# Dense down products with the two operands exchanged, summed into the same banks as the gathered rows, and tile 0 closed later

## What is computed

```python
def peer_ffn(xn, w_q, keys, U, V):
    ...                                  # top 16 of 128 x 128 product keys, 8 heads
    eidx = jnp.take_along_axis(cidx, sel, axis=-1)     # 128 experts of a token
    gate = jax.nn.softmax(top, axis=-1)
    def block(args):
        xb, eb, gb = args
        hid = jax.nn.gelu(jnp.einsum('nkd,nd->nk', U[eb], xb))
        return jnp.einsum('nk,nkd->nd', (hid * gb), V[eb])
```

## Time and profile before

| | us |
|---|---|
| median of 3 runs | 2242.39 |
| lowest, highest | 2233.48, 2247.92 |
| the profiled execution, device time | 2228.19 |
| its span, first to last instruction | 2226.1 |

### The profile page before, as it was taken

The page is one execution under the profiler, slowest core; times in us unless marked ns, Lnnn a source line. Parts: engine busy times, 40 slices in busy tenths (PEclk is TensorE's granted clock), DMA queues, the critical chain, the costliest instruction groups (busy, mean ns, idle before and its releaser), DMA issues.

```text
span 2226.1 us, 37936 instructions
## 1 busy us (share of the span) xinstructions
PE 2028.4 (91%) x13044; PEld 1240.7 (56%) x13044; DVE 1440.3 (65%) x3365; ACT 845.8 (38%) x2456; POOL 743.5 (33%) x658
## 2 busy tenths in 40 slices
PE   6998989989999888999989898899899997889997
PEld 5777768764444222444478776787544442234444
DVE  2425454569999898545542354744899989975545
ACT  1221222034545785433322203220444557853332
POOL 0400000025555676545312000000355457755552
PEclk9999999999999999999999999999999999999999
DMA  6330233658899999999753201436599999999995
GB/s 259 125 121 2 80 124 127 235 188 317 311 346 359 371 356 349 361 374 397 302 223 116 94 20 65 160 133 239 202 320 340 378 365 355 371 374 390 370 385 234
DMA packets 121546, 569.81 MB, mean 256 GB/s; under 512 B 42505, under 2 KB 44713, under 8 KB 61609
## 3 DMA queue, kind: packets, MB, share of 16 engines
q0 software_dynamic: 76032, 389.06, 46.6%
q1 hardware_dynamic: 43648, 175.12, 21.7%
q10 hardware_dynamic: 1696, 3.45, 0.4%
HBM read 725.63 MB, written 6.58 MB: 329 GB/s over the span
## 4 chain that ended last, share of the span: by engine, by line
PE 57%; DVE 24%; issue 9%; ACT 4%; DMA 4%; another core or an unknown queue 1%; POOL 0%; DVEq 0%; SPq 0%; ACTq 0%; POOLq 0%
PE ps L1059 12%; PE ps L978 11%; PE ps L585 10%; PE ps L648 7%; DVE arena L2019 6%; PE ps L936 3%; PE ps L905 3%; PE ps L919 3%; DMA arena<-in_uv,arena 2%; PE ps L1007 2%; DVE arena L2044 1%; DVE arena L1914 1%; DVE arena L1905 1%; DVE arena L1904 1%; DMA ring<-in_uv,arena 1%
## 5 line engine op out<-in xcount | busy, mean ns | idle before, releaser
L1471 POOL DMA_INDIRECT arena<-in_uv,arena x264 | 333.6, 1263 | 276.7 <-PE ps L978 237.7
L1471 POOL DMA_INDIRECT ring<-in_uv,arena x264 | 322.6, 1222 | 265.1 <-PE ps L978 219.2
L2019 DVE SCALAR_TENSOR_TENSOR arena<-arena 128x1024 bf16<-128x1024 f32 x264 | 319.4, 1224 | 113.1 <-DMA arena<-in_uv,arena 102.8
L2019 DVE SCALAR_TENSOR_TENSOR arena<-ring,arena 128x1024 bf16<-128x1024 f32 x264 | 320.2, 1225 | 111.7 <-DMA ring<-in_uv,arena 102.1
L978 PE MATMUL ps<-arena 64*64 64x512 f32 x2112 | 289.5, 619 | 46.6 <-ACT arena L1363 39.6
L978 PE MATMUL ps<-ring,arena 64*64 64x512 f32 x2112 | 291.0, 622 | 43.9 <-ACT arena L1363 39.0
L1361 ACT ACTIVATE arena<-arena 128x1 f32<-128x1 f32 x528 | 105.4, 200 | 494.7 <-DVE arena L2019 485.8
L1461 POOL COPY arena<-arena 128x8 uint32 (+1 forms) x66 | 37.1, 562 | 750.7 <-DVEq L1986 750.3
L1059 PEld LDWEIGHTS ps<-hold,ub 128*128 128x128 f32 x1024 | 180.5, 190 | 161.1 <-issue 143.6
L1059 PE MATMUL ps<-hold,ub 128*128 128x256 f32 x1024 | 268.9, 398 | 0.0
L648 PE MATMUL ps<-xn,ring 128*128 128x264 f32 x1024 | 246.1, 399 | 15.5 <-remote 12.8
(11 more groups left out here) (443 smaller groups left out, 2385.8 us busy)
## 6 DMA issues: line engine op xcount, KB each, us to landing
ring<-in_w SPq DMA_DIRECT2D x88, 1024.0 KB
ub<-in_uv SPq DMA_DIRECT2D x64, 512.0 KB
ub<-in_ud SPq DMA_DIRECT2D x48, 512.0 KB
hold<-in_ud SPq DMA_DIRECT2D x16, 512.0 KB, 6.0
ring<-in_uv,arena POOLq DMA_INDIRECT x264
arena<-in_uv,arena POOLq DMA_INDIRECT x264
hold<-in_st SPq DMA_DIRECT2D x2, 2048.0 KB
out_st<-hold SPq DMA_DIRECT2D x2, 2048.0 KB
```

Of the source, the lines that this page charges most:

```text
L1471: e.indirect_dma_start(out=row(k), out_offset=None, in_=A["uv"], in_offset=bass.IndirectOffsetOnAxis(ap=ix[:, par, k:k + 1], axis=0), **sk ...
L2019: stt(prod[:, n % 2, :], u, 1.0, xtok[:, tt, :], ALU.mult, ALU.mult, accum_out=hid[:, k:k + 1]).then_inc(S("dve_hid"), 1)
```

## The change

The down products exchange their operands: `hd` (64 or 128 tokens) becomes the weight and V moves with 512 columns, so that the result is token-major and goes to the banks of tile 0 (0, 1) and of tile 1 (2, 3), where the gathered rows are summed as well. In the bank of the second half the swapped halves ask for two products with 64 tokens each. A block is 6 products in four parts (`part` = 2 tt + half) in place of 8 in eight. Tile 0 stays open until the end of `down_slots`. The samples get banks 4 and 5, the sample sum at the end bank 6. `add_down`, the wait for `dve_xa` and the second opening of banks 0 and 1 go.

```diff
-SUM_BANK = (0, 2, 0)
+SUM_BANK = (0, 2, 4)
...
                     for s in range(n):
-                        if s == n - SLOT:
-                            e.wait_ge(S("dve_xa"), 1)
-                            open_sum(0, 1)
                         weighted(s % SLOT, 1 if s < n - SLOT else 2)
-                        for j, dt in [divmod(m_, KT) for m_ in range(s * DENSE * KT // n, (s + 1) * DENSE * KT // n)]:
-                            if dt == 0:
+                        for j, part in [divmod(m_, 2 * TT) for m_ in range(s * DENSE * 2 * TT // n, (s + 1) * DENSE * 2 * TT // n)]:
+                            if part == 0:
                                 take(e, w_full[j % UB], 16)
-                            m = mm(bank(4 + dt // 2, SEQ, SEQ * (dt % 2)), ub[:, j % UB, dt * P:dt * P + P], hd[:, j, :],
-                                   start=False, stop=False, skip_group_check=True)
-                            if dt == KT - 1:
+                            tt, half = divmod(part, 2)
+                            v = ub[:, j % UB, 512 * half:512 * half + 512]
+                            for q in range(1 + half):
+                                to = chunk(q) if half else slice(0, P)
+                                of = slice(tt * P + HD * (1 - q), tt * P + HD * (2 - q)) if half else slice(tt * P, tt * P + P)
+                                m = mm(ps[to, SUM_BANK[tt] + half, :], hd[:, j, of], v, start=False, stop=False, skip_group_check=True)
+                            if part == 2 * TT - 1:
                                 m.then_inc(w_free[j % UB], 1)
...
-                close_sum(0)
                 e.wait_ge(S("act_step"), step("act_it1"))
                 open_sum(2, 3)
-                gate_slots(1)
-                for half in range(2):
-                    turned(0, half, half + 1)
-                with e.Fori(0, 3) as i:
+                with e.Fori(0, 4) as i:
                     gate_slots(1)
...
-                open_sum(4, 5, 6, 7)
+                open_sum(4, 5)
                 down_slots()
-                mm(bank(7, 1), nothing, nothing[:, 0:1], start=False, stop=True, skip_group_check=True).then_inc(S("pe_step"), 1)
+                close_sum(0)
                 close_sum(2)
                 for k in range(SLOT):
                     weighted(k, 1)
+                    if k == 1:
+                        for half in range(2):
+                            turned(0, half, half + 1)
                     if k == 7:
                         sum_squares_first(l)
-                    if k == 3:
+                    if k == 4:
                         e.wait_ge(S("act_acc"), 4)
...
-                    if s == P + SLOT:
+                    if s == samples + 1:
                         sums_out(0, 1)
...
-                    if s == samples + 2:
+                    if s == samples + 3:
                         sums_out(2, 2)
...
-                    if s >= samples + 2 and s < samples + 6:
-                        add_down(s - samples - 2)
+                    if s in (samples + 4, samples + 5):
+                        add_turned(0, s - samples - 4, 1 + s - samples - 4)
```

More of the change, by code:

```diff
@@ L76 @@
 BIG = 3.0e38
-PE_STEPS = ("ket", "vt", "dl", "hy", "lr", "kk", "rk", "tr", "bv", "rot", "if", "rows", "svt", "sa", "po", "mean", "it0", "it1", "vd")
+PE_STEPS = ("ket", "vt", "dl", "hy", "lr", "kk", "rk", "tr", "bv", "rot", "if", "rows", "svt", "sa", "po", "mean", "it0", "it1")
 NORM_EPS, RWKV_EPS, HEAD_EPS = 1e-6, 64e-5, 1e-5
@@ L163 @@
 LATE = ("dve_hid pe_acc pe_xa act_acc act_top dve_top dve_route sp_sw sp_sr act_ps pe_ps pe_wq act_step pe_step "
-        "sp_out sp_fin sp_dfin dve_ix dve_xa").split()
+        "sp_out sp_fin sp_dfin dve_ix").split()
 ARENA = 22208
@@ L373, in build @@
                 "pe_cf pe_xt pe_cm pe_co pe_ctr pe_hh pe_ks pe_p pe_ps pe_s pe_sc pe_y pe_step pe_t pe_u pe_var pe_wo "
-                "pe_wq dve_hid pe_acc pe_xa act_acc dve_ix dve_xa "
+                "pe_wq dve_hid pe_acc pe_xa act_acc dve_ix "
                 "pool_hg pool_hy "
@@ L1104, in _ @@
                             from_ = NS // 2 * (kt // 4)
-                            m = mm(bank(0, NS, NS * kt), xtok[:, 2, kt * P:kt * P + P], C("group")[:, from_:from_ + NS], start=True, stop=True)
+                            m = mm(bank(6, NS, NS * kt), xtok[:, 2, kt * P:kt * P + P], C("group")[:, from_:from_ + NS], start=True, stop=True)
                         m.then_inc(S("pe_xa"), 1)
@@ L2064, in add_turned @@
                     own(i)
[L2066 to L2071, removed]
                 now = {}
@@ L2113, in _ @@
                         e.wait_ge(S("act_xt"), 3)
[L2114 to L2117, removed]
                     dot(s % P, s // P, s + (SLOT if s >= samples else 0), row_round + s // SLOT)
@@ L2120, in _ @@
                 e.wait_ge(S("pe_xa"), 3)
-                own(tt_(x[:, :, SEQ:N], x[:, :, SEQ:N], bank(0, NS * KT).rearrange("p (a b) -> p a b", b=NS), ALU.add))
+                own(tt_(x[:, :, SEQ:N], x[:, :, SEQ:N], bank(6, NS * KT).rearrange("p (a b) -> p a b", b=NS), ALU.add))
                 for half in range(2):
```

## The result

| | before | changed |
|---|---|---|
| median of 20 runs, us | 2235.4 | 2244.15 |
| lowest, highest | 2230.77, 2247.92 | 2235.35, 2251.02 |
| profiled execution's span | 2226.1 | 2234.2 |

The ratio is 1.0031, with a 95% interval of [1.0019, 1.0043]: slower by 0.3%, some 7 us (4 to 10). The forecast was +6.4 us, 0.3%, and 2248 in all. The 2248 stands 4 us above the median measured because it started from 2242.4, the median of three runs, and 20 runs of the kernel before have theirs at 2235.4. The medians differ by 8.75 us, the ratio says 7. A second measurement, with 10 runs of the changed kernel, gave 1.0022 [1.0002, 1.0042].

What follows compares the result with a forecast made beforehand. PE was taken to bound the down stage, DVE the gate stage and layer end. Terms 4.6 - 0.4 - 1.5 + 0.5 = +3.2 us a layer, +6.4 for two, gave 2248 us from 2242.4; range 2233 to 2264.

Steps and rivals of the forecast that it cites:

- What bounds the kernel: PE sets the down stage, full for 217.00 us; DVE sets the gate stage and the end of the layer.
- The down products: Down stage: 128 parts, wide ones at 1.06 us and pairs at 1.02, 133.1 in place of 128.5; +4.6 us a layer.
- the banks' opening: Down stage: the second opening of banks 0 and 1 leaves the middle of the stage; -0.4 us a layer.
- Rougher steps: Down stage: steps hold 1 or 2 parts where they had 2 or 3 products; costed at nothing.
- SP's clears: End of the layer: SP's 70 semaphore clears wait for tile 0's close, 11 us at most; costed at nothing.
- rows of V: Down stage: V blocks come at the same pace, with SP's queue unchanged there; no cost.
- The gate stage: Steps 96 to 167: tile 0's two additions leave DVE; -1.5 us a layer, bounds 0 and 1.69.
- The end of the layer: After the down products: DVE waits for tile 0's turned half, last dot at T + 10.55, before T + 10.07; +0.5 us.
- Serial pairs: Down stage: a pair's two products run one after the other, 1.90 us, 56 us more a layer, 2361 us; chance 0.04.
- A load showing in each pair: Down stage: each pair shows one more 0.13 us weight load, 8.4 us a layer, 2265 us; chance 0.06.
- Cheaper changes between neighbours of 128 rows: Down stage: form changes cost less, pair at 0.94, with DVE's full 1.69; -2.1 us a layer, 2238 us; chance 0.12.
- DMA as the bound: Down stage: DMA engines at 0.99 set it, hiding longer products and the gate stage's saving; 2242 us; chance 0.05.

Runs made afterwards that it cites:

- the kernel without the addition: Kernel before without tile 0's two additions in steps 142 and 143, the waits kept; down stage 217.82 us in both layers.
- fours: Kernel before with its own down products laid down in fours, 64 groups in place of 88; ratio 0.9969, stages 213.67 and 217.38 us.
- eights: Kernel before with the eight down products of a block in one group, 32 groups; ratio 0.9997, stages 216.15 and 217.69 us.

## Why the prediction was right, point by point

**What bounds the kernel.** As said. The control without a fifth of the traffic is the strongest sign: 221.85 us to the hundredth, with DMA at 0.91 in place of 0.98.

**The down products.** A 128-wide part was put at 1.06 and measured 1.06. The pair was put at 1.02 and measured 1.01. The term was +4.6 with the banks' opening of -0.4, together +4.2; measured 221.85 - 217.8 = +4.0 us in the first layer. In the second it was +2.4 by the profiles, where the old one had a first down step at half clock; the kernel without the addition gives that layer as 217.82, so +4.0 too. The clock of the old first steps of that layer:

```profile
1976.60:1981.00 4.40, 4.36 (x20) 1.62 (x20) 3.38 (x11) 1.69 (x6) 2.19 (x3) 0.61 1.03 406
```

Added up from start to start, the parts take 4.5 us more than the old products and the opening of the banks was 0.4. That the growth is the changes of form was argued in the prediction and is shown now: with 40 changes fewer and the same streamed columns the stage is 216.84, and with the very same products in another order 216.3 to 217.0, waits and half clock included.

**Rougher steps, SP's clears, rows of V.** Nothing, as costed: no weighted step waited for ACT in either down stage behind the first.

**The gate stage.** -1.5 was taken between 0 and -1.69. The dots show the 1.70 from the old rows on DVE: dot 140 to 146 fell from 13.28 to 11.58 us in both layers of the changed kernel. From step 128 to 168 it came, in the first two profiles, to -1.7 in the first layer and -0.6 in the second; over all runs, as above, to -1.9 and -0.4. So the source was right and the size was not the same in both layers: the mean is -1.1, and in the second layer the gathers take most of it back, which the prediction had named as its bound of 0.

**The end of the layer.** +0.5 was forecast, measured +0.2: the last dot at T + 10.25 in place of T + 10.55. The chain was the one described, link by link: ACT's copies at T + 0.4, the held-back gelu, the weighted step at T + 2.46 (T + 2.5), the transposes, the addition at T + 4.17 (T + 4.3). The rest is rounding in DVE's items.

**Sum.** By stages +4.0 - 1.7 + 0.2 = +2.5 us in the first layer and, with the clock's stretch taken out of the old down stage, +4.0 - 0.6 + 0.2 = +3.6 in the second, 6.1 in all against 6.4 forecast. The ratio's 7 us (4 to 10) hold that. That the sum is so near is in part luck: for both layers together the down stage grew by 0.4 us less than forecast and the end by 0.6 less, and the gate stage gave back 0.7 less (0.8 over all runs).

**The rivals.** Serial pairs: shown false (276.35 us). A load showing in each pair: false, a pair is 1.01 us and a load of 0.13 more would show. The Trainium skill, "TensorE: Matmul & The Clock Gate", section "The mechanism" of Part 3, has the rule that would ask for it, in its list of what overlaps; the trace does not agree with that rule for these pairs. The same section also has loads into the background weight buffer pulled ahead, and nothing here speaks against that. Cheaper changes between neighbours of 128 rows: false, a step of a wide part and a pair takes 2.06 us, a step of two wide parts 1.91. The Trainium skill, "TensorEngine Tiling (Array Packing)", section "Key Properties", says that changing the tiling mode drains the array. No row shows the drain itself; the trace agrees in that a group behind a change costs more than its streamed columns: a second wide part in a group adds 1.91 - 1.06 = 0.85 us, so the change is some 0.2 us in the 1.06 of a wide part, and some 0.15 in the 1.01 of a pair. DMA as the bound: false for this kernel, true for the fours and eights just below it.

**What the forecast missed**, though it cost no number: how near the second bound is. At 217.8 us the old stage had no wait, but each order with fewer groups waits in one layer or both, at stage lengths from 212 to 219 us. By these lengths some 4 us were left above the second bound in the first layer and almost none in the second; that is an estimate, since stretches at half clock lie in most of them.

## What to carry to other kernels

Where PE is full from end to end, count changes of form (128 wide, pairs of 64 wide) beside streamed columns: each costs 0.15 to 0.2 us for float32 work of this size, and an order of the same products with fewer of them takes PE's time down (here 7 to 14 us a layer, of which 0.4 to 9.8 arrived). An exchange of operands that halves the weight loads gains nothing if these lie under moving data already. Before paying for such a gain, look at the next engine's share: a DMA share of 0.99 beside a full PE was harmless, but of the 8 us that PE gave back in the fours only 4 arrived in the first layer and under 1 in the second, stretches at half clock included.

## What was unexpected

The spread of whole runs (2231 to 2248 us for one kernel) goes with PE's granted clock in stretches that the change doesn't touch: over the first layer's mixers, the same instructions, it was 0.97 in four profiled executions and 0.94 to 0.96 in nine, and the first weighted step started at about 493 us in the former and mostly at 498 to 502 in the latter. Down stages without a wait and at full clock repeat to the hundredth (217.82 three times, 221.85 five times); the two stages of the same kernels that differ (219.46 and 223.44 us) began at half clock. The regrouped kernels have both such stretches and waits.
